# Eight gate modulations of the second modulated layer, moved from layer one's pairs into layer three's attention

## The reference, cut to what matters

```
cond = silu(c)
mod = cond @ ada_w[l] + ada_b[l]            # 3 * 1024 numbers for layer l
shift, scale, gate = split(mod, 3)
h = rms_norm(x, norm_g[l]) * (1 + scale) + shift
...                                         # layer l makes out from h
x = x + gate * out
```

## Time and profile before

| | us |
|---|---|
| median of three runs | 1765.78 |
| lowest, highest | 1763.6, 1766.76 |
| the profiled execution, its own time | 1764.11 |
| span of the profile | 1762.4 |

### The profile page before, as it was taken

How to read it: one execution, slowest core, us unless ns; L and a number is a source line. 1 busy time by engine, 2 the same in 40 slices (tenths; PEclk the granted TensorE clock), 3 DMA queues, 4 the chain that set the end, 5 groups by cost and what they waited for, 6 DMA issues and landing times.

```text
span 1762.4 us, 38758 instructions
## 1 busy us (share of the span) xinstructions
PE 1664.6 (94%) x16172; PEld 1267.4 (72%) x16172; DVE 1235.5 (70%) x2231; ACT 806.0 (46%) x1505; POOL 795.9 (45%) x713
## 2 busy tenths in 40 slices
PE   5899999999989899999999999999999999999997
PEld 5677776777776668757777777787777778777766
DVE  7578878988879788269997777535887436355553
ACT  3544444454443273365544444434767433444443
POOL 3534334344342245457883222544545545544433
PEclk9999999999999999999999999999999999999998
DMA  7212311312313123212221111123222232433312
GB/s 305 95 63 74 110 54 70 121 51 74 121 51 133 38 96 125 96 48 73 84 96 49 37 37 37 61 96 108 72 84 71 82 99 81 140 115 117 109 57 90
DMA packets 51902, 155.12 MB, mean 88 GB/s; under 512 B 5888, under 2 KB 12032, under 8 KB 51600
## 3 DMA queue, kind: packets, MB, share of 16 engines
q1 hardware_dynamic: 51728, 152.65, 25.6%
HBM read 150.50 MB, written 2.13 MB: 87 GB/s over the span
## 4 chain that ended last, share of the span: by engine, by line
PE 66%; DVE 20%; ACT 5%; issue 4%; POOL 2%; DVEq 0%; POOLq 0%; ACTq 0%
PE bank L524 16%; PE bank L528 14%; PE bank L525 14%; PE bank L1272 7%; PE bank L2360 3%; DVE ya L1599 2%; DVE best L2468 2%; DVE lru_xc L2852 2%; DVE score L2471 2%; PE bank L3077 1%; PE bank L1230 1%; PE bank L2390 1%; PE bank L3092 1%; DVE probs_t L2515 1%; PE bank L570 1%
## 5 line engine op out<-in xcount | busy, mean ns | idle before, releaser
L498 POOL TENSOR_TENSOR w_lo<-raw,w_hi 128x512 fp32r<-128x512 f32 (+2 forms) x434 | 578.6, 1349 | 603.2 <-ACT w_hi L480 591.7
L524 PE MATMUL bank<-h_hi,w_hi 128*128 128x512 f32 x1368 | 578.1, 423 | 10.2 <-ACT h_hi L973 2.5
L528 PE MATMUL bank<-h_lo,w_hi 128*128 128x512 f32 x1368 | 543.3, 397 | 10.8 <-DVE h_lo L941 6.3
L525 PE MATMUL bank<-h_hi,w_lo 128*128 128x512 f32 x1368 | 541.5, 396 | 0.0
L480 ACT ACTIVATE w_hi<-raw 128x512 fp32r<-128x512 f32 (+2 forms) x434 | 248.1, 603 | 252.7 <-PE bank L528 172.0
L524 PEld LDWEIGHTS bank<-h_hi,w_hi 128*128 128x128 f32 x1368 | 260.9, 191 | 100.2 <-issue 34.0
L528 PEld LDWEIGHTS bank<-h_lo,w_hi 128*128 128x128 f32 x1368 | 260.7, 191 | 77.1 <-DVE h_lo L941 11.4
L525 PEld LDWEIGHTS bank<-h_hi,w_lo 128*128 128x128 f32 x1368 | 261.5, 191 | 57.4 <-issue 9.3
L1599 DVE SCALAR_TENSOR_TENSOR ya<-padded,vecs,ya 128x512 f32<-128x512 f32 x240 | 214.2, 893 | 3.9
L3153 DVE CUSTOM_DVE_ANT_0 fox_probs<-bank,fox_keybias 128x128 f32<-128x128 f32 (+3 forms) x64 | 28.9, 488 | 84.7 <-PE bank L3077 84.4
L524 PE MATMUL bank<-own_hi,w_hi 128*128 128x512 f32 x208 | 82.9, 398 | 1.6 <-ACT own_hi L973 1.6
(11 more groups left out here) (412 smaller groups left out, 2826.8 us busy)
## 6 DMA issues: line engine op xcount, KB each, us to landing
raw<-even_in SPq DMA_DIRECT2D x57, 512.0 KB, 3.7
raw<-odd_in SPq DMA_DIRECT2D x39, 512.0 KB, 3.2
raw<-ada SPq DMA_DIRECT2D x32, 512.0 KB, 4.0
raw<-fox_in SPq DMA_DIRECT2D x25, 512.0 KB, 3.3
raw<-lru_in SPq DMA_DIRECT2D x24, 512.0 KB, 3.2
ada_first<-ada SPq DMA_DIRECT2D x16, 512.0 KB, 13.7
raw<-even_out SPq DMA_DIRECT2D x16, 512.0 KB, 3.3
raw<-odd_out SPq DMA_DIRECT2D x16, 512.0 KB, 3.3
```

The source lines that it names most:

```text
L498: e.tensor_tensor(k.w_lo[s % NSPLIT][:, at], k.raw[n % NRAW][:, at], k.w_hi[s % NSPLIT][:, at].bitcast(F32), ALU.subtract).then_inc(*did(" ...
L524: e.matmul(out, hi[:, w], x[i][0], start=start and i == 0, stop=False, skip_group_check=True)
L525: e.matmul(out, lo[:, w], x[i][0], start=False, stop=False, skip_group_check=True)
L528: m = e.matmul(out, hi[:, w], x[i][1], start=False, stop=stop and i == kt - 1, skip_group_check=True)
```

## The change

The 16 shift and scale columns of layer two stay in layer one, two in each pair (2p and 2p + 1). The eight gate columns, 16 to 23, leave the pairs: `ada3` is gone from VectorE's lists, and the pair's three remaining modulations are `ada0`, `ada1`, `ada2`. Columns 16 and 17 are now loaded behind the block of g3, 18 and 19 behind g4, 20 and 21 behind g5, 22 and 23 behind g6; VectorE does them at `gate_times(g)[0]` and 0.8 tiles later. The norm of layer two waits for 16 columns in place of 24.

```
@@ plan_weights
                 even(3 * DT + p + 1)
-                ada(1, [3 * p])
+                ada(1, [2 * p])
                 even(5 * DT + p + 1)
-                ada(1, range(3 * p + 1, 3 * p + 3))
+                ada(1, [2 * p + 1])
                 even(DT + p + 1, p + 1)
                 even(6 * DT + 1 + p)
             else:
                 even(6 * DT + 1 + p)
                 ada(0, [2 * DT + p])
-                ada(1, range(3 * p, 3 * p + 3))
+                ada(1, [2 * p, 2 * p + 1])
...
         for h in range(AH):
             add(("g", h), "odd_in", AH + 2 + IH // 2 + h)
+            ada(1, late_gates(h))
...
+def late_gates(g):
+    return range(2 * DT + 2 * (g - 3), 2 * DT + 2 * (g - 2)) if 3 <= g < 3 + DT // 2 else ()
@@ the lists of VectorE: "ada3^", "ada3" and "ada3" are taken out
-        tap19^ chain1^ chain2^ ada2^ chain3^ kk_norm^ tap20^ ada3^ chain4^ A^ chain5^ B^ r_lerp^ chain6^ R^ U^ rk^
+        tap19^ chain1^ chain2^ ada2^ chain3^ kk_norm^ tap20^ chain4^ A^ chain5^ B^ r_lerp^ chain6^ R^ U^ rk^
...
@@ even_vector
     def modulations(p, at):
-        for n, (layer, j) in enumerate(((0, 2 * DT + p), (1, 3 * p), (1, 3 * p + 1), (1, 3 * p + 2))):
+        for n, (layer, j) in enumerate(((0, 2 * DT + p), (1, 2 * p), (1, 2 * p + 1))):
@@ odd_vector
-                [("made", "mod", 1, j) for j in range(3 * DT)],
+                [("made", "mod", 1, j) for j in range(2 * DT)],
...
+    def modulations(g):
+        for n, j in enumerate(late_gates(g)):
+            yield gate_times(g)[0] + 0.8 * n
+            modulate_raw(k, e, need, did, 1, j)
...
-          chain(*(gate_out(g, gate_times(g)[-1] + 0.3) for g in range(3, AH))))
+          chain(*(s for g in range(3, AH) for s in (modulations(g), gate_out(g, gate_times(g)[-1] + 0.3)))))
```

More of the change, by code:

```diff
@@ L1130 @@
         tap11 tap12 tap13 tap14 tap15 merge1 tap16 PAt tap17 G tap18 C tap19 chain1 chain2 ada2 chain3 kk_norm tap20
-        ada3 chain4 A chain5 B r_lerp chain6 R U rk v_lerp tap21 tap22 tap23 tap24 V""",
+        chain4 A chain5 B r_lerp chain6 R U rk v_lerp tap21 tap22 tap23 tap24 V""",
     "scalar": """
@@ L1148 @@
     "vector": """
-        tV ada0 mm0 mm1 N N_t val_done' tap25' ada1 ada2 ada3 f_norm tap26' tap27' tB tap28' tap29' tap30' sq1
+        tV ada0 mm0 mm1 N N_t val_done' tap25' ada1 ada2 f_norm tap26' tap27' tB tap28' tap29' tap30' sq1
         f_out tap0 tap1 sq2 sq2p tap2 tap3 tap4 tap5 sq3p tap6 tap7 tap8 tap9 tap10 tap11 sq4 turn0 merge0 tap12 tap13
```

## The result

| | before | after |
|---|---|---|
| median, us | 1764.92 (4 runs) | 1772.7 (4 runs, 1770.6 to 1775.06) |
| ratio, 95% interval | | 1.005 [1.0032, 1.0067] |
| profiled execution, span, us | 1764.11, 1762.4 | 1775.06, 1773.3 |
| VectorE busy, us | 1235.5 | 1238.1 |

The kernel became 7.8 us slower, where the forecast was +3.4 (1769.2 in the range 1763 to 1773.5). The sign was right, the size was not. The two profiled executions lie 10.9 us apart.

A forecast was written before the change was run, and what follows sets the result against it. TensorE was read as 66% of the chain of waits and VectorE 20%, so a modulation counts only where VectorE is on the chain. Terms 0 - 2.6 + 2.6 + 3.4 = +3.4 us gave 1769.2, range 1763 to 1773.5.

The forecast's parts named there:

- Pairs 0 to 6: Layer one: removing one modulation per pair only lengthens VectorE's wait for TensorE at chain6, 0 us.
- The ring: Raw-block loads in layer one's pairs: one stop fewer per pair ends ScalarE's 8.1 us load wait, costed at nothing.
- The last pair: Last pair of layer one: VectorE gains 0.9 us ahead of the transpose and the clock 1.7, -2.6 us.
- the clock's 1.7: Last pair, behind TensorE's wait: with the idle time halved, most of 1.7 us lost to a low clock comes back.
- Group 0: Attention, first eight tiles: four added modulations cost 4.3 us, less 1.7 of clock, +2.6 us, bounds 1.9 and 6.6.
- The clock's -1.7: Attention's first group: the low clock falls into earlier waits, where VectorE hides it, -1.7 us.
- Group 1: Attention, up to tile 15: four added modulations cost 1.7 us of delay and 1.7 of clock, +3.4, bounds 0 and 6.1.
- 20 and 21 hidden: Columns 20 and 21, just behind group 0's `attended`: VectorE waits there, so no cost; otherwise up to 2 x 1.33 us.
- Lock and clock add up: Rival: group 0 costs 4.9 and keeps its low clock, group 1 3.4, last pair gives 0.9: +7.4, 1773.2 us; 22%.
- Hidden after all: Rival: the eight modulations vanish in VectorE's 40 us of idle time in the attention, 1763.2 us; 8%.
- the ring frees the pairs: Rival: TensorE's 0.8 us wait for `w_lo` per pair goes with the late load, 5.6 us, 1763.6 us; 10%.
- A pair changes its length: Rival: a shift of tenths turns one layer-one pair over, 2.5 us either way, 1766.7 or 1771.7 us; 18%.

The follow-up runs named there:

- e1: Changed kernel's layer-one pairs, the eight gate modulations done nowhere (columns filled with the bias), against the kernel before: 1765.26 us, ratio 1.0008.
- e3: Changed kernel with all eight gate modulations moved behind tile 16 of the attention: 1764.03 us, ratio 0.9999 to the kernel before.
- e8: Changed kernel with four gate modulations at tile times 9.43, 10.23, 14.0 and 14.8, the rest behind tile 24: 1766.9 us, ratio 1.0019 to before.
- e7b: Changed kernel, but GpSimd writes zeros into `w_lo` for blocks g4, g5, g6 instead of subtracting: 1768.12 us, ratio 1.0021 to the kernel before.
- e4: Changed kernel with its first four gate modulations in place and the other four moved to tile times 25.5 to 43.5: 1768.28 us, ratio 1.002 to before.
- e5b: Changed kernel with two gate modulations at tile times 14.0 and 14.8, the rest behind tile 24: 1764.54 us, ratio 1.0 to the kernel before.
- e6b: Changed kernel with two gate modulations at tile times 9.43 and 10.23, the rest behind tile 24: 1764.66 us, ratio 1.0 to the kernel before.
- e2: Kernel before, all modulations in the pairs, with the eight gate modulations done a second time in the attention at the changed kernel's places: 1774.41 us, ratio 1.0053.
- e10: Kernel before with only column 23 taken out of the last pair and made at tile time 17.5 in the attention: 1763.88 us, ratio 1.0003.

## Why the prediction was right in sign and wrong in size

**Pairs 0 to 6, forecast 0: held, one step earlier than said.** VectorE's waits for TensorE in the recurrence of the fourth pair were 0.72 us before (328.88, 339.02) and are 2.49 now. Timeline of VectorE after:

```profile
329.68 0.28 DVE L1695 SCALAR_TENSOR_TENSOR S<-bank,carry,S 128x64 f32<-128x64 f32 x1 [0.46 <-PE bank L1277]
...
334.06 0.28 DVE L1695 SCALAR_TENSOR_TENSOR S<-bank,carry,S 128x64 f32<-128x64 f32 x1 [1.09 <-PE bank L1277]
...
335.91 0.28 DVE L1695 SCALAR_TENSOR_TENSOR S<-bank,carry,S 128x64 f32<-128x64 f32 x1 [0.24 <-PE bank L1277]
...
339.82 0.28 DVE L1695 SCALAR_TENSOR_TENSOR S<-bank,carry,S 128x64 f32<-128x64 f32 x1 [0.45 <-PE bank L1277]
...
341.35 0.76 DVE L1700 TENSOR_TENSOR W<-bank,W 128x256 f32<-128x256 f32 x2 [0.25 <-PE bank L1277]
```

The gain of 1.54 us (column 11, a scale, was made here before; another pair makes it now) became 1.77 us of waiting. Most of it comes at `chain4`, the step right behind the removed modulation; I had named `chain6`.

**The ring: held.** ScalarE's wait of 8.1 us for a load is gone, and TensorE's 0.8 us for `w_lo` are still there. Waits after, 286 to 352 us (who for whom: total, times, longest):

```profile
ACT w_hi L485 <- PE bank L533: 4.7, 2, 4.1
...
PEld bank L529 <- POOL w_lo L503: 0.8, 1, 0.8
```

**The last pair, forecast -2.6: about 0, the first failed term.** VectorE's part was read rightly (the wait 1.74 became 0.84; 24.31 became 23.20). What failed is the step "TensorE resumes 0.9 us earlier", and with it the clock's 1.7 behind it as a thing to count on. TensorE does start its batch earlier, but a pause of 1.07 to 1.92 us without releaser stands behind the wait in after and in each of the nine experiments in which at least one modulation fewer stands ahead of that wait.

The traces say what the pause is tied to. The DMA queue q8, of kind "instruction", moves 128 blocks of 16 KB in the execution, about one for every 250 of TensorE's matmuls and weight loads (16172 of each). In after one of them is under way from 572.00 to 573.27 us:

```profile
q8 instruction: 1, 0.02, 6.1%
```

(DMA queues, window 572.0 to 573.3: packets, MB, share of 16 engines.) The pause begins at 573.29, and the product behind it starts 1.35 us after the block's end. Such a block stands at this place in all twelve traces, and the same product, the 18th of its batch, starts 1.27 to 1.51 us after its end in every one, before included (block 568.47 to 569.62, product 570.98): there the wait for VectorE covered it. So it looks as if TensorE's next instructions bound this place as well, and VectorE's gain could move it only a little. No run moved the block: this is a match of times in twelve traces and not a test.

The clock then came out either way. Eight traces have the changed kernel's orders in layer one (after, e1, e3 to e8). From 545.6 to 583 us, 37.31 before, after, e1, e7b and e8 are 0.3 to 0.5 us longer; e3, e4, e5b and e6b, where the granted clock behind the pause was 1.00, are 1.2 to 1.5 us shorter. So in single executions half of the -2.6 is sometimes there, and e1's median (+0.8 us, interval -0.2 to +3.0) leaves no room for all of it. That after shows none is in part luck of this execution.

**Group 0, forecast +2.6, measured +3.4.** With GpSimd's reads taken away (e7b) it costs 2.84, which is the forecast's 4.0 for three modulations less the 1.2 that the divide gets back. The subtractions then lengthen column 16 by 0.6 (1.84 against 1.22) and column 18 by 0.8 + 0.9, together 2.3, and 2.84 + 2.3 = 5.1. I had 4.3, and 4.9 as the bound: I took only the one meeting that the trace before showed, and column 16 met the subtractions as well. The clock's -1.7 came as forecast (7.27 to 5.59), and in the forecast's way: the low clock now lies in front of `attended` (0.58 from 946 to 950 us).

**Group 1, forecast +3.4, measured +5.2: the second failed term.** The working for columns 22 and 23 is right when they stand there without group 0's load: e8 has +3.1, a wait of 1.85 (forecast 2.0) and 1.6 of clock (a size that e7b, with the same wait and no fall, shows to be one of two outcomes). What failed is "20 and 21 hidden": not so when group 0 is loaded, too. They are hidden when TensorE is slow behind group 0 (e6b, e8: the wait grows by nothing from them), and when they aren't lengthened (e7b: clock kept, wait 1.85). With the clock kept and the subtractions in them, VectorE can't follow: its idle time between the two groups is 0.75 us in the changed kernel, against 1.5 in e8 and 7.7 before, and TensorE's wait is 2.66 in the changed kernel and 2.64 in e2: 0.8 us more than in e8. So half of the 1.7 us of clock that I booked as a gain at group 0 was given back at the next deadline. The rest, 1.3 us, is that the clock stayed low for longer (8.85 against 7.57 in e2 behind the same wait); why, the runs don't settle.

**The rivals.** "Lock and clock add up" named 1773.2 and the median is 1772.7, but by another sum: the last pair gave nothing instead of 0.9, group 0 did recover its clock, and group 1 cost more than that rival had. "Hidden after all" and "the ring frees the pairs" fell (e2, and the waits above). "A pair changes its length" is real in single profiles and averages out as far as can be told: e1, with the changed pairs, stands at +0.8 us, not told apart from 0.

In sum: 0 (pairs) + 0 (last pair) + 3.4 + 5.2 = 8.6 us in the profile, where the medians say 7.8. The prediction's chance of "slower" was also summed wrongly: its own parts (22, half of 42, and 9) give 52%, not 47.

## What to carry to other kernels

Moved work isn't free because its engine idles somewhere later. It is free where that engine waits for the bottleneck at that moment (e3: eight modulations for nothing), and it costs its full time ahead of a deadline such as the last tile of a group. A gain that makes the bottleneck faster at one deadline has to be carried forward to the next one, where the other engine may not keep up. Where the bottleneck waits for one engine, look also at what else arrives at that time, its own instructions included, before the wait is booked as a gain. And an overlap with another engine's memory reads that is seen once in the trace has to be counted for each moved instruction, not once.

## What the runs showed of the hardware

A VectorE add of a single 128x1 column takes 0.16 us, and 1.09 to 1.22 us when GpSimd subtracts 128x512 tiles beside it (the last pair of after has 1.22 at 553.75, beside two subtractions that began at 553.69); with a memset in place of the subtraction it takes 0.16. Behind the same TensorE wait of 1.94 to 1.95 us, 32 equal matmuls took from 2.01 to 3.69 us in eight kernels (2.01 in e5b, 2.50 in e10, 3.68 before). And taking 0.8 to 1.25 us of a visible wait away from TensorE brought an unlabelled one of 1.07 to 1.92 us, whose end came 1.27 to 1.51 us after the landing of a 16 KB block of instructions; here the wait in the profile was only an upper bound of what its removal gave.
